# First block of a two-block fp32 layer kernel: a computed step order with half projections, modulation weights loaded row by row, weight ring loaded in halves

## What is computed

```python
def first_block(x, ln_g, w_in, qk_g, sinks, w_branch, w_out, rel_bias):
    hn = rms_norm(x, ln_g[l])
    proj = jnp.einsum('bsd,dc->bsc', hn, w_in[l])          # 23 chunks of up to 512 columns
    (qa, ka, va, ga, qb, kb, vb, gb, qc, kc, vc, gc, gate_logits) = jnp.split(proj, SPLIT_POINTS, axis=-1)
    # q and k: rms_norm per head of 64, then three attentions of 8 heads each
    # o_a: one block of keys; o_b: three groups (1, 4, 16 dilated) with one softmax over all; o_c: window and sinks
    br = jnp.einsum('bsiw,iwd->bsid', branches, w_branch[l])
    merged = jnp.sum(jax.nn.sigmoid(gate_logits...) * br, axis=2)
    x = x + jnp.einsum('bsd,de->bse', merged, w_out[l])
# second block
ada = jax.nn.silu(c) @ w_ada + b_ada                      # [1024] @ [1024, 6144]: the modulation
# then norm, projections, attention over 64 selected keys, w_out, router, mixture of 64 experts
```

## Time and profile before

| | |
|---|---|
| median of three runs | 1200.89 us (1199.4 to 1202.67) |
| the profiled execution | 1205.1 us, its span 1203.2 us |
| mean granted TensorE clock | 0.909 |
| busy, share of the span | PE 88%, weight loads 70%, DVE 67%, ACT 48%, POOL 16% |
| first matmul of a projection | 19.6 us |
| end of the last branch product of the first block | 517.5 us |
| moved from HBM | 244.38 MB, 205 GB/s over the span |

### The profile page before, as it was taken

One profiled execution on the slowest core, in us unless ns is written; L12 is line 12 of the kernel. 1 busy time (PEld: TensorE's weight loads), 2 busy tenths in 40 slices (PEclk: granted clock), 3 DMA queues, 4 the chain that ended last, 5 costly groups with the idle time before them and its releaser, 6 DMA issues.

```text
span 1203.2 us, 15830 instructions
## 1 busy us (share of the span) xinstructions
PE 1055.8 (88%) x4992; PEld 845.3 (70%) x4992; DVE 800.7 (67%) x1332; ACT 582.5 (48%) x887; POOL 194.8 (16%) x235
## 2 busy tenths in 40 slices
PE   4998679985999899986897967879999999999995
PEld 3876568765766666655775956658888888888883
DVE  3656566767542744245669654368889898999995
ACT  4555343423332233232434431247777777777773
POOL 3022110010000000001113000123232323232230
PEclk9999888985799798987889977979999999999997
DMA  8443547666252630632432311468888888888882
GB/s 277 173 169 117 214 144 268 236 204 218 84 175 92 236 145 10 235 140 63 167 119 104 129 70 36 168 269 331 305 338 305 342 303 334 313 334 315 319 331 101
DMA packets 89248, 247.68 MB, mean 206 GB/s; under 512 B 11292, under 2 KB 21973, under 8 KB 75762
## 3 DMA queue, kind: packets, MB, share of 16 engines
q1 hardware_dynamic: 82914, 226.71, 51.7%
q0 software_dynamic: 6000, 19.96, 4.5%
q10 hardware_dynamic: 288, 0.40, 0.1%
HBM read 244.38 MB, written 2.68 MB: 205 GB/s over the span
## 4 chain that ended last, share of the span: by engine, by line
PE 42%; DVE 6%; issue 2%; DMA 2%; ACT 1%; POOL 0%; POOLq 0%; DVEq 0%; ACTq 0%
PE bank L1894 14%; PE bank L1921 7%; PE bank L1879 5%; PE bank L1642 5%; PE bank L1871 3%; DMA x_gathered<-h_rows,block_tokens 2%; PE bank L1639 2%; PE bank L1799 1%; PE bank L1861 1%; DVE w_lo L1098 1%; PE bank L1791 1%; PE bank L1909 1%; DVE score L1422 1%; PE bank L1806 1%; DVE top L1421 0%
## 5 line engine op out<-in xcount | busy, mean ns | idle before, releaser
L1642 PE MATMUL bank<-w_hi,a_hi 128*128 128x512 f32 (+2 forms) x512 | 215.4, 421 | 27.2 <-DVE w_lo L1098 16.2
L1642 PE MATMUL bank<-w_lo,a_hi 128*128 128x512 f32 (+2 forms) x512 | 208.4, 407 | 0.0
L1642 PE MATMUL bank<-w_hi,a_lo 128*128 128x512 f32 (+2 forms) x512 | 207.6, 405 | 0.0
L1098 DVE TENSOR_TENSOR w_lo<-ring,w_hi 128x1024 fp32r<-128x1024 f32 (+2 forms) x136 | 155.5, 1179 | 61.4 <-ACT w_hi L819 57.6
L819 ACT ACTIVATE w_hi<-ring 128x1024 fp32r<-128x1024 f32 (+2 forms) x140 | 138.2, 1021 | 95.8 <-PE bank L1642 72.9
L1519 DVE TENSOR_TENSOR up_lo<-raw_weights,up_hi 128x1024 fp32r<-128x1024 f32 x136 | 163.0, 1239 | 0.0
L1642 PEld LDWEIGHTS bank<-w_hi,a_hi 128*128 128x128 f32 x512 | 105.5, 206 | 58.9 <-issue 35.7
L974 ACT ACTIVATE up_hi<-raw_weights 128x1024 fp32r<-128x1024 f32 x136 | 136.3, 1053 | 5.2 <-DMA raw_weights<-in_w_dram 5.2
L1642 PEld LDWEIGHTS bank<-w_hi,a_lo 128*128 128x128 f32 x512 | 104.6, 204 | 22.1
L1642 PEld LDWEIGHTS bank<-w_lo,a_hi 128*128 128x128 f32 x512 | 105.0, 205 | 20.0 <-issue 0.5
L669 POOL TENSOR_SCALAR mean_squares<-mean_squares 128x8 f32<-128x8 f32 (+2 forms) x32 | 6.3, 197 | 655.0 <-ACT logits L774 359.5
(11 more groups left out here) (255 smaller groups left out, 1885.3 us busy)
## 6 DMA issues: line engine op xcount, KB each, us to landing
raw_weights<-in_w_dram SPq DMA_DIRECT2D x102, 1024.0 KB, 7.0
ring<-in_w_in_dram SPq DMA_DIRECT2D x29, 2048.0 KB, 8.1
ring<-in_w_ada_dram SPq DMA_DIRECT2D x12, 2048.0 KB, 9.1
ring<-in_w_out_dram SPq DMA_DIRECT2D x4, 2048.0 KB, 7.7
ring<-in_w_branch_dram SPq DMA_DIRECT2D x3, 2048.0 KB, 12.3
bias<-rel_rows SPq DMA_DIRECT2D x40, 128.0 KB, 8.1
block_rows<-place_rows SPq DMA_DIRECT2D x34, 128.0 KB, 8.8
ring<-in_ws_dram SPq DMA_DIRECT2D x3, 1024.0 KB, 4.9
```

The lines of the kernel that those rows point to most:

```text
L1098: dve.tensor_tensor(w_parts[1][:, 2 * p:2 * p + 2, 0:w], view(JOB[it[1:3]], kind)[:, 2 * p:2 * p + 2, :], w_parts[0][:, 2 * p:2 * p + 2, 0 ...
L1642: mm = pe.matmul(ps[:, 0:w], a_parts[za][:, k, t * P:(t + 1) * P], w_parts[zw][:, k, 0:w], start=start, stop=stop)
```

## The change

It does these things:

- `first_block` writes the list of the first block by a small planner instead of `FILL` and `SUMS`. A main line of projections and branch products is taken in order; every other step has a lag after the step it depends on (`SCALE_LAG`, `TURN_LAG`, ...) and is put in ahead of the main line when that lag is over by the planner's own prices (`PE_US`). Chunk 13 now comes before chunks 10 to 12.
- A projection is two steps of 12 matmuls, `half` and `proj`; other steps can stand between them. Two of the four pieces of the next chunk are emitted after each.
- The scaling by the inverse root becomes a step `scale_rows`, and the exponential a step `exp`, both later in the list than the step that feeds them. `msum` and `rstd` get two alternating parts (and a third for the norms), `nmax`, `den` and `rden` eight instead of four, and one-unit heads use three `logits` and `probsT` places per parity.
- `w_ada` no longer passes through the ring: 96 rows of 256 KB go through four places in `G`, loaded three rows ahead; a row is asked for when the row four before it has been added.
- Each ring slot is loaded as two halves of 1 MB, each asked for when the same half of the job two before it has been split. `w_branch` jobs load in halves too.
- Before the second block begins, the first pieces of `w_out` are split during the last gate projection and not after the last branch product.

The core of the diff:

```diff
--- before.py
+++ after.py
-FILL = [3] * 4 + [2] * 4 + [2, 1, 2] + [2, 2, 2, 1, 1] + [0, 2, 1, 1, 1, 1, 1, 0]
-
-SUMS = {n: 4 for n in range(1, 11)} | {16: 8}
...
+def first_order():
+
+    chunks = [2, 3, 0, 1, 4, 5, 6, 7, 8, 9, 13, 10, 11, 12, 14, 15, 16]
+    steps = []
     for c in chunks:
         for t in range(NT):
-            groups.append([("proj", c, t)] + ([pending] if pending else []))
-            pending = ("turn", c, t) if CHUNKS[c][0] in ("q", "k", "kv") else None
+            steps += [("half", "proj", c, t), ("proj", c, t)]
     for i in range(3):
         for hf in range(2):
             for t in range(NT):
-                groups.append([("proj", len(chunks) + 2 * i + hf, t)])
-            for t in range(NT):
-                groups.append([("branch", i, hf, t)])
-    return groups
+                steps += [("half", "proj", len(chunks) + 2 * i + hf, t), ("proj", len(chunks) + 2 * i + hf, t)]
+            steps += [("branch", i, hf, t) for t in range(NT)]
+    return steps
+
+
+N_ROWS = N_ADA * KT
+ADA_SLOTS = 4
+
+def first_block():
+
+
+    PE_US = {"half": 2.7, "proj": 2.7, "turn": 0.45, "score": 1.0, "score_rest": 1.0, "flip": 0.35, "value": 0.75,
+             "turn_branch": 1.6, "branch": 3.8, "ada_out": 1.0}
+    s, end, now = [], {}, 0.0
+    main = first_order()
...
+    def ready(it):
+        kind = it[0]
+        if kind == "scale_rows":
+            return after(it[1:], SCALE_LAG)
+        if kind == "turn":
+            return max(after(("scale_rows", "proj") + it[1:], TURN_LAG), last_turn + BANK_LAG)
+        if kind == "score":
+            n = it[1]
+            need = {0: 1, 8: 9, 16: 15}.get(n)
+            at = last_score + UNIT_EVERY[n // 8]
+            return max(at, after(("turn", need, 1), 2.5)) if need else at
+        if kind == "score_rest":
+            return after(("score", it[1]), 0.0 if len(units_of(it[1])) == 1 else 3.0)
+        if kind == "exp":
+            return after(("score_rest", it[1]), 3.0 if len(units_of(it[1])) == 1 else 4.0)
+        if kind == "flip":
+            return after(("exp", it[1]), 4.0 if len(units_of(it[1])) == 1 else 5.0)
+        if kind == "value":
+            n = it[1]
+            need = {0: ("proj", 3, 1), 8: ("proj", 12, 1), 16: ("proj", 16, 1)}.get(n)
+            at = max(after(("flip", n), 3.0 if len(units_of(n)) == 1 else 4.0), last_value + 3.0)
+            return max(at, after(need, 4.0)) if need else at
+        if kind == "turn_branch":
+            at = max(after(("value", 8 * it[1] + 7), 5.0), last_turn + BANK_LAG)
+            return max(at, after(("branch", it[1] - 1, 1, 1), 0.5)) if it[1] else at
+        if kind == "ada":
+            return ADA_FROM + ADA_EVERY * (KT * it[1] + it[2])
+        if kind == "ada_out":
+            return max(after(("ada", it[1], KT - 1), 5.0), last_turn + BANK_LAG)
+        if kind == "branch":
+            return max(after(("turn_branch", it[1]), 2.0), after(("ada", N_ADA - 1, KT - 1), 0.0))
+        return 0.0
+
+    order = ("scale", "turn", "exp", "value", "flip", "score", "ada", "ada_out")
+    while main or any(queue.values()):
+        if len(main) == len(first_order()) - 6 and ("small",) not in s:
+            s.append(("small",))
+        it = next((queue[k][0] for k in order if queue[k] and ready(queue[k][0]) <= now), None)
+        if it:
+            for k in order:
+                if queue[k] and queue[k][0] == it:
+                    queue[k].pop(0)
+        elif main and ready(main[0]) <= now:
+            it = main.pop(0)
+        else:
+            now = min([ready(queue[k][0]) for k in order if queue[k]] + [ready(it) for it in main[:1]])
+            continue
+        s.append(it)
...
+SCALE_LAG, TURN_LAG, BANK_LAG = 4.5, 2.5, 3.0
+UNIT_EVERY = (9.0, 15.0, 6.0)
+ADA_FROM, ADA_EVERY = 24.0, 2.5
...
+            lo, hi = (0, PIECES // 2) if it[0] == "half" else (PIECES // 2 if ("half",) + main in steps else 0, PIECES)
+            ahead = {("out1", 1, 1): PIECES // 2, ("proj2", 7, 1): 0}.get(it, hi)
+            s += [("split",) + nxt + (p,) for p in range(lo, ahead)]
...
+        if it[0] == "proj2" and CHUNKS2[it[1]][0] in ("q2", "k2", "kiwi"):
+            s.append(("scale_rows",) + it)
...
-    s = [("start",)]
+    s = [("start",)] + first_block()
...
-    def head(n, k, m=0):
...
-        msum = sb("mean_squares", [P, 8])
-        rstd = sb("rstd", [P, 8])
-        nmax = sb("neg_max", [P, 4, 2])
-        den = sb("den", [P, 4, 2])
-        rden = sb("rden", [P, 4, 2])
+        msum = sb("mean_squares", [P, 3, 8])
+        rstd = sb("rstd", [P, 3, 8])
+        nmax = sb("neg_max", [P, 8, 2])
+        den = sb("den", [P, 8, 2])
+        rden = sb("rden", [P, 8, 2])
...
-            return L[:, n % 2] if n < 24 else L[:, h % 2, h // 2 % 2:h // 2 % 2 + 1]
+            return L[:, n % 2] if 8 <= n < 16 else L[:, n % 2, n // 2 % 3:n // 2 % 3 + 1]
...
+        def ada_row(q):
+
+            at = q % ADA_SLOTS
+            return G[:, at // 2, at % 2 * CH:at % 2 * CH + CH]
+
+        def half_ready(eng, j, h):
+
+            eng.wait_ge(S(f"ring_loaded_{j % RING}_{h}"), 16 * len(range(j % RING, j + 1, RING)))
...
+                        whole = split_kind(*last[1:3])[1] == CH
+                        sp.wait_ge(S("w_lo"), PIECES * SPLITS.index(last[1:3]) + (2 * h + 2 if whole else PIECES))
+                rows = slice(KT // 2 * h, KT // 2 * h + KT // 2)
+                if kind in ("w_in", "w_in_2"):
+                    _, c0, w, _ = {"w_in": CHUNKS, "w_in_2": CHUNKS2}[kind][arg[0]]
+                    src = a[kind][0].rearrange(d_rows, k=KT)[:, rows, c0:c0 + w]
+                    sp.dma_start(view(j, split_kind(kind, arg[0])[0])[:, rows, :], src).then_inc(done, 16)
...
+            def load_ada(q):
+
+                if q >= ADA_SLOTS:
+                    c, k = (q - ADA_SLOTS) // KT, (q - ADA_SLOTS) % KT
+                    if k < KT - 1:
+                        sp.wait_ge(S("ada_step"), (KT - 1) * c + k + 1)
+                    else:
+                        sp.wait_ge(S("ada_summed"), c + 1)
+                else:
+                    sp.wait_ge(S("x_scaled"), NT)
+                c, k = q // KT, q % KT
+                src = a["w_ada_2"][0].rearrange(d_rows, k=KT)[:, k, CH * c:CH * c + CH]
+                sp.dma_start(ada_row(q), src).then_inc(S(f"ada_loaded_{q % ADA_SLOTS}"), 16)
...
+                if it[0] == "small":
+                    sp.wait_ge(S("rel_ready"), 1)
+                    sp.dma_start(rel_dram, relrow).then_inc(S("rel_stored"), 16)
+                    sp.wait_ge(S("rel_stored"), 16)
+                    for u in range(BIAS_SLOTS - 1):
+                        load_bias(u)
+                    for q in range(ADA_SLOTS - 1):
+                        load_ada(q)
...
+                if it[0] == "ada" and KT * it[1] + it[2] + ADA_SLOTS - 1 < N_ROWS:
+                    load_ada(KT * it[1] + it[2] + ADA_SLOTS - 1)
+                if it[0] == "split" and it[3] % 2 and JOB[it[1:3]] + RING < len(JOBS):
+                    load_half(JOB[it[1:3]] + RING, it[3] // 2)
...
-                if it[0] == "score_rest":
+                if it[0] == "exp":
...
+                if kind0 == "scale_rows":
+                    m, t = NTH_NORM[it[1:]], it[3]
+                    kind, _, _, dst = (CHUNKS if it[1] == "proj" else CHUNKS2)[it[2]]
+                    nh = {"kv": 2, "kiwi": 1}.get(kind, 8)
+                    dve.wait_ge(S("head_rstd"), m + 1)
+                    r8 = bc(rstd[:, m % 2, 0:nh], HD)
+                    dve.wait_ge(S("rows_copied"), m + 1)
+                    if kind in ("q", "k"):
+                        o = qn[:, m % 2, :].rearrange("p (h d) -> p h d", d=HD)
+                        dve.tensor_tensor(o, o, r8, ALU.mult).then_inc(S("normed"), 1)
...
-                        if m >= 1:
-                            dve.wait_ge(S("head_rstd"), m)
+                        if m >= 2:
+                            dve.wait_ge(S("head_rstd"), m - 1)
...
-                        dve.wait_ge(S("head_rstd"), m + 1)
...
+                    _, c, k = it
+                    q = KT * c + k
                     o = ada_acc[:, c % 2, :]
-                    w = view(j, "k8")
-                    if part == 0:
-                        job_ready(dve, j)
+                    dve.wait_ge(S(f"ada_loaded_{q % ADA_SLOTS}"), 16 * (q // ADA_SLOTS + 1))
...
+                    begins = first_half or it not in HALVED
+                    ks = range(KT) if it not in HALVED else range(KT // 2) if first_half else range(KT // 2, KT)
+                    ps = use_bank(n) if begins else proj_b[n % 2]
...
```

336 lines of the change are left out of this document (148 added, 188 removed).

## The result

| | before | the change |
|---|---|---|
| median | 1201.78 us (1199.4 to 1203.65, four runs beside the change) | 1144.84 us (1143.88 to 1146.02) |
| ratio, 95% interval | | 0.952 [0.9502, 0.9538] |
| span of the profiled execution | 1203.2 us | 1142.4 us |
| mean granted TensorE clock | 0.909 | 0.936 |
| end of the last branch product | 517.5 us | 459.5 us |

The kernel is 57 us faster; 1157 was forecast, and 1130 to 1190 held it. In the profiled executions 58.0 of the 60.8 us come out of the first block.

The account below looks back on a forecast made before the run. The first block was taken as bound by PE and its waits. Idle −38, clock −9, start +4, after the block −1 sum to −44: 1161 for the profiled execution, 4.2 above the median, so 1157 us; range 1130 to 1190.

Parts of the forecast that it names:

- What bounds the block: First block: bound by PE and what makes it wait; time after the last branch product stays about 686 us.
- −1: After the first block: `out1` starts with its pieces already made, 1 us less.
- Idle time: PE's 56.9 us idle in the first block falls by 38 us: `w_lo` waits, turns with short waits, and flips.
- The 8.9 us of `w_lo`: PE's waits for `w_lo` in the first block all go, with the ring in halves and without `w_ada`: −8.9 us.
- The flips: PE's 12.7 us of waits for probability copies: the longest, 5.3, goes; 7.4 in 6, of dilated heads, stay.
- The turns and short waits: PE's waits for `kT` and `qT` copies, 19.4 us, and short ones, 15.9: 24 of the 35 us come back.
- The clock: Low clock on the first block's projection matmuls costs 17 us, of which 9 come back; bounds nothing and 17.
- the work itself is 424 us: PE's 441 us busy in the first block, less 17 us of low clock on projections.
- The scaling's wait: DVE's 2.04 us wait for POOL's inverse root, 18 times, leaves its queue; counted at nothing since DVE isn't the bound.
- Rival 2: DVE becomes the bound while `w_ada` rows are added; at most 74% busy, the stretch takes 277 us: 1184; chance 0.19.
- Rival 3: `w_ada` rows land too late, three per turn of landing plus 1.1 us, setting the pace from 6.7: 1210; chance 0.07.
- The start: First rows of `w_ada` queue behind other loads and come late, so PE loses 4 us.

Follow-up runs that it names:

- old_list: The change with the first block's old order put back, new buffers, ring halves and row loads kept: 1217.30 us, ratio 1.0138.
- exp_early: kv_late with the exponential 2 us earlier in the list, the flip as far behind the score as before: 1134.99 us, ratio 0.9442.
- kv_late: The change, but behind the one narrow chunk both halves of the next ring load are asked for after its last piece: 1137.76 us, ratio 0.9463.
- lead_1: kv_late with rows of `w_ada` loaded one ahead, not three, in the same four places: 1199.18 us, ratio 0.9982.
- no_halves: The change with every half step taken out, projections run in one piece of 24 matmuls, list not planned anew: 1173.91 us, ratio 0.9783.
- scale_at_once: The change with each scaling of q and k rows put right behind its projection: 1157.90 us, ratio 0.965.
- lead_2: kv_late with rows of `w_ada` loaded two ahead, not three, in the same four places: 1153.32 us, ratio 0.9562.
- ring_whole: The change with both halves of a ring slot asked for together, after the old chunk's last piece is split: 1140.33 us, ratio 0.9488.
- kv_prices: kv_late with two planner prices set to the trace, turn 0.5 us and 16-matmul `ada_out` 2.1 us: 1141.87 us, ratio 0.9492.
- few_tiny: The change with seven eighths of the one-column modulation sums left out, so output is not the layer's: 1046.61 us; block ends at 443.5 us.

## Why the prediction was right, and where not

- **What bounds the block: right.** PE's waits and its low clock were the pool, and the rest of the program stayed: 682.9 us behind the last branch product, 686 ± 5 predicted; the 2.8 us less stand against −1.
- **Idle time: right in sum, in part by luck in its terms.** −37.3 us measured; −38 less 4 of new waits predicted. The 8.9 us of `w_lo` went. The flips gave 8.8 in place of 5.3: "they stay", I said of 7.4 us in 6, and 3.9 us in 7 are left. The turns and short waits gave less than the 24 that I took: 35.3 us before, 15.7 after, so 19.6, and 5.2 of what is left is the gap at 261. Nor did the `w_lo` waits go by the ring alone, to which I had put them: old_list frees the ring as well and keeps 6.6 of the 8.9. The part of each edit is not cleanly separable, since the waits move into one another; the added buffers, chunk 13's place and the early pieces of `w_out` were not tried by themselves.
- **The clock: the term that was mis-sized.** "−9 of 17" against 21.3 us measured. The pool was too small: "the work itself is 424 us" counted low clock on projection matmuls alone. The same matmuls took 411.7 us in exp_early, so some 29 of before's 441.1 us went with the low clock. The projections did about as forecast: the mean record of one pass fell from 408 to 400 ns, by the prediction's scale (0.400 − 0.390) / 0.24 = 4.2% of 1104 at the low level or 9 us, so 8 of 17 came back. The other 13 are mostly the small matmuls of heads, which I had taken at the durations they had, low clock included. (The turns and the one-column sums stayed: 12.4 and 12.5 us, 16.5 and 16.6.)

Two groups of small matmuls in the block (busy us, mean ns), before and then after:

```profile
L1784 PE MATMUL bank<-V,probsT 128*128 128x64 f32 x240 | 34.0, 294 | 1.9 <-ACT probsT L951 1.9
L1736 PE MATMUL bank<-kT,qT 64*128 64x256 f32 x80 | 27.9, 434 | 0.0
```

```profile
L1860 PE MATMUL bank<-V,probsT 128*128 128x64 f32 x240 | 30.9, 278 | 0.0
L1812 PE MATMUL bank<-kT,qT 64*128 64x256 f32 x80 | 23.7, 383 | 0.0
```

They fell by 3.1 and 4.2 us; with the flips (22.6 to 20.1) and the other score form (21.0 to 18.4) that is 12.4 in records, which overlap.

- **What brings the low clock: both sides hold.** PE's busy time goes down with its idle time (windows from 20 us to the block's end; the five versions from kv_late on stand in their own table):

| | PE idle, us | PE busy, us | clock | low projections |
|---|---|---|---|---|
| old_list | 67.2 | 444.3 | 0.88 | 80 |
| before | 56.9 | 441.1 | 0.89 | 78 |
| lead_1 | 51.5 | 441.4 | 0.91 | 95 |
| no_halves | 37.5 | 427.7 | 0.93 | 81 |
| scale_at_once | 28.7 | 423.3 | 0.94 | 63 |
| lead_2 | 27.4 | 422.3 | 0.95 | 65 |
| the change | 19.6 | 419.9 | 0.95 | 45 |
| ring_whole | 16.8 | 419.5 | 0.96 | 51 |

  A straight line through all thirteen rises by 0.6 us of busy time for each us of waiting. It is no law: kv_prices and exp_early have the same idle time (13.9 and 14.0) and differ by 10 us in busy time and by 38 low projections. The orders differ too, so that idle time is the cause is not shown by the table. The Trainium skill ("TensorE: Matmul & The Clock Gate", section "HAM oscillation — how this bites in real kernels") has idle gaps as the cause, and this table agrees with it in the main. It is not the whole of it here: few_tiny has a low spell behind its gap of 5.93 us, and shows too that nearly all low projections of 512 columns left in the change came behind one-column matmuls, without a gap. The prediction had such spells remain "8 times"; the change has five.
- **The scaling's wait "at nothing": wrong.** 13 us (scale_at_once). I took DVE as not the bound, being busy 277 of 498 us. The wait did leave DVE's queue, so the term was a gain that I left out. For the change packs DVE: busy 81.1 of the 100 us from 100 on, with PE busy 98.3, and in such a stretch waits of 2 us, 18 times, would land on PE. The prediction named the condition ("if DVE became dense they would count") and didn't ask whether it would hold.
- **Rival 2: its ceiling of 74% was no ceiling.** The stretch ran with 184.0 / 250 = 74% over all, but the densest 100 us stood at 81% with PE hardly idle. The rows took from 49 to 317 us, some 17 more than the 250 that the rival's sum has; what part of that is DVE's was not tested apart.
- **Rival 3: landing forecast right, law wrong.** Some 5 us were expected and 5.2 measured, under the 6.7 from which rows would set the pace. But the pace isn't three rows a turn, nor does SP trail DVE's last addition (lead_1). Of DVE's 18.3 us of waits for rows the longest, 6.9, came from SP standing at a ring load; the others were not traced one by one, and kv_late still has 17.2. The Trainium skill ("DMA: Bandwidth & Descriptors", section "Bandwidth") says to batch to 1 MiB or more, for the sake of the rate; here 96 loads of 256 KB stand beside a faster kernel, landing as fast at the median as the 1 MB ones beside them (5.2 and 5.1 us). The fixed 2 us a load that the prediction quotes was not measured here by itself.
- **Halves.** The prediction gave them no term of their own, only "at least 12 matmuls between". Without them the same list is 29 us slower, half of the gain, though part of that is the lags that shrink with them (no_halves).
- **The start.** +4 us was charged; from 20 to 100 us PE is idle 2.1 us, as it was before (77.89 busy of 80, before 77.87). That, the clock's 12 us and 2 us behind the block are why the sum of −44 stands against −60.8. All three erred to one side.
